# A transformer trunk with routed experts on one core: the 32-slot expert round moved into the last stored round, gate projections regrouped, filler matmuls added

## The reference, cut to what matters

```python
logits = (h @ router).astype(jnp.float32)
top_v, top_i = lax.top_k(logits, TOP_K)          # TOP_K = 2 of N_EXPERTS = 8
w = jax.nn.softmax(top_v, axis=-1)
combine = jnp.sum(jax.nn.one_hot(top_i, N_EXPERTS, dtype=jnp.float32) * w[..., None], axis=-2)
gu = jnp.einsum('btd,edf->btef', h, w_gu)        # w_gu: 8 x 1024 x 2816
g, u = jnp.split(gu, 2, axis=-1)
act = jax.nn.silu(g) * u * combine[..., None].astype(h.dtype)
return jnp.einsum('btef,efd->btd', act, w_down)  # w_down: 8 x 1408 x 1024
```

## Time and profile before

| | |
|---|---|
| median of 3 runs | 2147.89 us (2145.49 to 2149.15) |
| the profiled execution's own time | 2149.53 us |
| its span, first to last instruction | 2147.7 us |
| mean granted TensorE clock | 0.986 |
| busy: PE, PEld, DVE, ACT, POOL | 2078.1, 1535.5, 826.7, 381.4, 126.9 us |
| DMA | 550.71 MB, mean 256 GB/s |

### The profile page before, as it was taken

How to read it: one execution, slowest core, us unless ns; L and a number is a source line. 1 busy time by engine, 2 the same in 40 slices (tenths; PEclk the granted TensorE clock), 3 DMA queues, 4 the chain that set the end, 5 groups by cost and what they waited for, 6 DMA issues and landing times.

```text
span 2147.7 us, 44261 instructions
## 1 busy us (share of the span) xinstructions
PE 2078.1 (97%) x19281; PEld 1535.5 (71%) x19281; DVE 826.7 (38%) x1886; ACT 381.4 (18%) x816; POOL 126.9 (6%) x221
## 2 busy tenths in 40 slices
PE   6998999999999999999999999999998999999998
PEld 4776878888899655456587688888887876554564
DVE  2235753777575500101312345653336734001013
ACT  1124441000110110001132310001134331110010
POOL 3100010111000000000100011110000000000000
PEclk8999999999999999999999999999999999999999
DMA  9974039997546599999885799844441038999997
GB/s 337 280 261 138 13 100 323 349 298 265 195 154 221 204 367 401 397 393 398 301 246 189 256 341 293 284 127 139 137 137 56 13 102 325 365 400 399 394 394 266
DMA packets 376942, 550.71 MB, mean 256 GB/s; under 512 B 13104, under 2 KB 328880, under 8 KB 371424
## 3 DMA queue, kind: packets, MB, share of 16 engines
q1 hardware_dynamic: 349888, 466.59, 62.2%
q0 software_dynamic: 21968, 77.10, 10.8%
q10 hardware_dynamic: 4896, 4.21, 0.6%
HBM read 537.90 MB, written 14.67 MB: 257 GB/s over the span
## 4 chain that ended last, share of the span: by engine, by line
PE 88%; DVE 6%; DMA 2%; ACT 2%; issue 1%; ACTq 0%; SPq 0%; DVEq 0%
PE ps L731 85%; DMA work<-in_ada_w 2%; DVE ring L2270 1%; DVE ring L2264 1%; ACT ring L1670 1%; DVE ring L2245 1%; ACT work L1670 1%; DVE ring L2289 1%; DVE work L2103 1%; PE ps L1304 1%; PE ps L921 0%; DMA ring<-in_ada_w 0%; PE ps L1244 0%; PE ps L1190 0%; DVE ring L2278 0%
## 5 line engine op out<-in xcount | busy, mean ns | idle before, releaser
L731 PE MATMUL ps<-hT,ring 128*128 128x256 f32 (+1 forms) x2912 | 637.7, 377 | 2.8 <-DVE hT L2113 2.5
L731 PE MATMUL ps<-ring,work 128*32 128x352 f32 (+5 forms) x7320 | 618.3, 438 | 8.6 <-ACT work L1670 5.7
L731 PEld LDWEIGHTS ps<-hT,ring 128*128 128x128 f32 x2912 | 542.9, 192 | 102.9 <-issue 20.5
L731 PEld LDWEIGHTS ps<-ring,work 128*32 128x32 f32 (+2 forms) x7320 | 307.0, 116 | 291.6 <-issue 196.2
L1670 ACT ACTIVATE work<-ps 128x256 f32<-128x256 f32 (+13 forms) x244 | 104.6, 433 | 1254.9 <-PE ps L731 992.2
L731 PE MATMUL ps<-work,ring 128*128 128x256 f32 (+2 forms) x1664 | 322.0, 352 | 1.1 <-DVE work L2397 0.9
L731 PEld LDWEIGHTS ps<-work,ring 128*128 128x128 f32 (+1 forms) x1664 | 275.3, 187 | 35.6 <-issue 1.6
L2754 DVE SCALAR_TENSOR_TENSOR work<-work,csil 128x1024 f32<-128x1024 f32 x196 | 239.5, 1280 | 45.3 <-DMA work<-in_ada_w 45.0
L731 PE MATMUL ps<-ring 64*64 64x64 f32 (+1 forms) x4192 | 153.3, 235 | 18.4 <-DVE ring L2289 9.1
L2621 DVE TENSOR_TENSOR work<-work,ps 96x352 f32<-96x352 f32 (+2 forms) x72 | 37.4, 520 | 322.1 <-PE ps L731 321.6
L731 PEld LDWEIGHTS ps<-ring 64*64 64x64 f32 x4192 | 130.4, 139 | 33.1 <-DVE ring L2289 13.8
(11 more groups left out here) (294 smaller groups left out, 1253.4 us busy)
## 6 DMA issues: line engine op xcount, KB each, us to landing
ring<-in_moe_w_gu SPq DMA_DIRECT2D x128, 1408.0 KB, 13.8
work<-in_ada_w POOLq DMA_DIRECT2D x112, 512.0 KB, 6.3
ring<-in_moe_w_down SPq DMA_DIRECT2D x48, 1024.0 KB, 13.0
ring<-in_ff_w_gu SPq DMA_DIRECT2D x88, 512.0 KB, 7.8
ring<-in_ada_w SPq DMA_DIRECT2D x40, 1024.0 KB, 7.9
ring<-in_dn_w_in SPq DMA_DIRECT2D x32, 1024.0 KB, 5.5
ring<-in_moe_w_down SPq DMA_DIRECT2D x64, 512.0 KB, 11.3
ring<-in_ff_w_down SPq DMA_DIRECT2D x44, 512.0 KB, 8.9
```

What stands on the lines that cost most here:

```text
L731: return pe.matmul(out, lhsT, rhs, start=start, stop=stop, **kw)
```

## The change

The 32-slot round is computed inside the last stored round: its gate columns stand before down chunks 4 to 7, its up columns before chunk 8, its turn before chunk 9 and its down product after chunk 10. Its rows stay in the chip (`y_tiny`, `back_tiny`), and the 128-slot round's scatter adds them by a second matmul behind each of its own. The 32-slot expert is now fetched seventh, the 128-slot one eighth. `xg_tiny` and its copy go. The gate projection makes `wab` stationary in groups of 32 columns, `hT` moving, and a second step sums the groups (`fold`). One panel of the attention layer goes ahead of the scores' waits, and fillers are added at the start, in the router, and at the end of DeltaNet. The counts in the semaphore waits follow (not shown), as do a new constant, memory for it (`par` shrinks), and a clear of `y_tiny` at the end of `wide` on VectorE.

```diff
@@ SP: the order in which experts are fetched
-                    n_end = sp.snap(n_last + TINY)
+                    n_more = sp.snap(n_last + (NARROW - 1))
...
                     next_expert(NARROW - 3, LAST_LARGE, for_large)
-                    with sp.Fori(TINY, n_end) as r:
-                        next_expert(r, r + (NARROW - TINY), [0, 1, 2, 3, 4, 5, 6, 7])
-                    next_expert(n_end, TINY, [0, 1, 2, 3, 4, 5, 6, 7])
+                    next_expert(NARROW - 2, TINY, [0, 1, 2, 3, 4, 5, 6, 7])
+                    with sp.Fori(NARROW - 1, n_more) as r:
+                        next_expert(r, r + 1, [0, 1, 2, 3, 4, 5, 6, 7])
@@ TensorE: body, the last stored round
                     if upcoming is not None:
                         pe.wait_ge(moe["d_g"], upcoming + (i + 1))
                         gather(0, G_pair)
-                    down(q, 4, 8, 3, first)
-                    if upcoming is not None:
+                        down(q, 4, 8, 3, first)
                         gather(1, G_pair)
                         gather(2, G_pair)
-                    down(q, 8, 11, 4, first)
+                        down(q, 8, 11, 4, first)
+                    else:
+                        columns_tiny(q + 1, GATE, 0)
+                        down(q, 4, 8, 3, first)
+                        columns_tiny(q + 1, UP, 1)
+                        down(q, 8, 9, 4, first)
+                        turn_tiny(q + 1)
+                        down(q, 9, 11, 4, first)
+                        down_tiny(q + 1)
@@ TensorE: scatter of the 128-slot round
+                        r = slice(BLK * b, BLK * (b + 1))
                         for c in range(2):
                             k = 2 * b + c
-                            ins = mm(ps[:, b, c * NT:(c + 1) * NT], y_w[:, k * P:(k + 1) * P], back_T)
+                            mm(ps[:, b, c * NT:(c + 1) * NT], y_w[:, k * P:(k + 1) * P], back_T, True, False)
+                            ins = mm(ps[:, b, c * NT:(c + 1) * NT], y_tiny[r, c * P:(c + 1) * P], back_tiny[r, :], False, True)
@@ TensorE: the end of experts
                 with pe.Fori(0, n_last) as r:
-                    wide(q0 + STORED + r)
-                tiny(pe.snap(q0 + n_last + STORED))
+                    wide(q0 + NARROW + r)
@@ ScalarE: tiny, which now also has the last stored round's output and stores
                     ins.then_inc(moe["a_at"], 4)
+                    act.wait_ge(moe["p_bt"], q - (6 * i + 5))
+                    f(back_tiny[:], ps[:, 1, NT:2 * NT], ACT.Copy).then_inc(moe["a_bt"], 1)
+                    output(q - 1, STORED * (i + 1) - 1)
+                    store(q - 1, LAST_LARGE)
                     act.wait_ge(moe["p_dn"], q * 4 + 4)
@@ VectorE: tiny
                     ins.then_inc(moe["d_act"], 2)
+                    output(q - 1, STORED * (i + 1) - 1)
                     dve.wait_ge(moe["p_dn"], q * 4 + 4)
-                    cp(y_tiny[64:P, :], ps[64:P, 4, 0:QUARTER]).then_inc(moe["d_y"], 1)
-                    for b in range(4):
-                        dve.wait_ge(moe["p_sc"], (q - STORED * (i + 1)) * 4 + (b + 1))
-                        residual(l, b, b, 40, moe["d_res"])
+                    cp(y_tiny[64:P, :], ps[64:P, 6, 0:QUARTER]).then_inc(moe["d_y"], 1)
@@ TensorE: the gates of DeltaNet (gates_in after unit 1, gates_folded after unit 2)
                     pe.wait_ge(small_in, SMALL[l])
+                    for k in range(KC):
+                        q = slice(BLK * (k % 4), BLK * (k % 4 + 1))
+                        ins = mm(ps[q, 6, 0:NT], wab[:, k, :], hT[:, k, :], k < 4, k >= 4)
+                    ins.then_inc(p_ab, 1)
+
+                def gates_folded():
+                    pe.wait_ge(d_ab, i + 1)
                     for g in range(2):
-                        for k in range(KC):
-                            mm(ps[:, 6, 32 * g:32 * g + 32], hT[:, k, g * P:(g + 1) * P], wab[:, k, :],
-                               k == 0, k == KC - 1)
-                    mm(ps[:, 6, 64:96], ones[0:1, :], arow[0:1, :]).then_inc(p_ab, 1)
+                        mm(ps[:, 6, NT + 32 * g:NT + 32 * g + 32], GATES(l)[:, g * P:(g + 1) * P], fold)
+                    mm(ps[:, 6, NT + 64:NT + 96], ones[0:1, :], arow[0:1, :]).then_inc(p_ab, 1)
@@ VectorE: the copy between them (gates_in of VectorE goes from w == 2 to w == 3)
+                    if w == 1:
+                        dve.wait_ge(p_ab, 3 * i + 1)
+                        cp(GATES(l), ps[:, 6, 0:NT]).then_inc(d_ab, 1)
@@ TensorE: fillers; end of DeltaNet, router, start of layer 0
                     sums(l, 8 + m, 2 + m % 2, ones)
+                    keep_warm(6, 1)
...
+                    if k < KC - 1:
+                        keep_warm(0, 1)
                 ins.then_inc(moe["p_rt"], 1)
...
-                    for _ in range(EARLY):
+                    for x in range(EARLY):
                         ada(0, 1, ROWS512(0))
+                        if x >= EARLY - 3:
+                            keep_warm(6, 3)
...
                     ins.then_inc(p_pro, 1)
+                    keep_warm(6, 3)
                     ada_turn(1, ROWS512(0))
+                    keep_warm(6, 4)
@@ TensorE: attention, one panel (NA_FIRST = 1, NA_PANELS[0] from 1 to 0)
+                pe.wait_ge(d_ct, 2)
+                pe.wait_ge(d_ar, ada_turned[0])
+                for _ in range(NA_FIRST):
+                    ada(NA_ACC, NA_ACC, ROWS512(l, True))
                 pe.wait_ge(a_pj, PJ0[l] + 12)
```

More of the change, by code:

```diff
@@ L51 @@
 C_RCAP = C_CAP + 2 * P
-NCONST = C_RCAP + COLS
+C_FOLD = C_RCAP + COLS
+NCONST = C_FOLD + 32
 def shape_constants():
@@ L204, in trunk @@
         identc = cst[:, C_IDC:C_IDC + HB]
+        fold = cst[:, C_FOLD:C_FOLD + 32]
         def level(l):
@@ L355, in trunk @@
         NA_ACC = 7
-        NA_PANELS = [1, 3, 2, 2, 0, 3, 3, 2, 0, 0]
+        NA_FIRST, NA_PANELS = 1, [0, 3, 2, 2, 0, 3, 3, 2, 0, 0]
         NA_WARM = [0, 0, 0, 0, 0, 0, 0, 0, 0, 5]
         NA_DONE, NA_TURN = (3, 7), (4, 8)
-        assert sum(NA_PANELS) == NA_CORE
+        assert NA_FIRST + sum(NA_PANELS) == NA_CORE
         PJ0 = {0: 0, 1: 12, 2: 24, 3: 36}
@@ L1497, in turn_tiny @@
                 def turn_tiny(q):
-                    pe.wait_ge(moe["d_res"], (q - STORED * (i + 1)) * 4 + 4)
-                    pe.wait_ge(moe["d_bk"], q - (STORED * (i + 1) - 1))
+                    pe.wait_ge(moe["d_bk"], q - (6 * i + 5))
+                    pe.wait_ge(moe["d_act"], q * 4 + 2)
                     for g in range(2):
-                        ins = pe.transpose(ps[:, 1, g * P:(g + 1) * P], back[:, g, :], ident)
+                        ins = pe.transpose(ps[:, 1, NT + g * P:NT + (g + 1) * P], back[:, g, :], ident)
                     ins.then_inc(moe["p_bt"], 1)
-                    pe.wait_ge(moe["d_act"], q * 4 + 2)
-                    for x in range(4):
+                    for x in (2, 3, 0, 1):
                         n = min(P, REACH - x * P)
-                        ins = pe.transpose(ps[0:n, 0 if x < 2 else 5, x * P:(x + 1) * P], ma[:, x * P:x * P + n], ident)
+                        ins = pe.transpose(ps[0:n, x // 2, (x % 2) * P:(x % 2 + 1) * P], ma[:, x * P:x * P + n], ident)
                     ins.then_inc(moe["p_tr"], 4)
@@ L1516, in down_tiny @@
                         for g in range(4):
-                            ins = mm(ps[BLK * g:BLK * (g + 1), 4, 0:QUARTER], ma_tiny_T[:, c, :], quarter(c, g),
+                            ins = mm(ps[BLK * g:BLK * (g + 1), 6, 0:QUARTER], ma_tiny_T[:, c, :], quarter(c, g),
                                      n == 0, n == 10)
                         down_done(ins, n)
-                def scatter_tiny(q):
-                    pe.wait_ge(moe["a_bt"], q - (STORED * (i + 1) - 1))
-                    for b in range(4):
-                        pe.wait_ge(moe["d_y" if b >= 2 else "a_y"], q + 1)
-                        r = slice(BLK * b, BLK * (b + 1))
-                        for c in range(2):
-                            ins = mm(ps[:, b, c * NT:(c + 1) * NT], y_tiny[r, c * P:(c + 1) * P], back_T[r, :])
-                        ins.then_inc(moe["p_sc"], 1)
-                def tiny(q):
-                    pe.wait_ge(moe["d_xt"], i + 1)
-                    columns_tiny(q, GATE, 7)
-                    columns_tiny(q, UP, 6)
-                    turn_tiny(q)
-                    down_tiny(q)
-                    scatter_tiny(q)
                 def body(q, upcoming, first=False):
@@ L2012, in experts @@
                 body(STORED - 1, None)
-                output(q0 + (STORED - 1), STORED * (i + 1) - 1)
-                store(q0 + (STORED - 1), LAST_LARGE)
+                tiny(q0 + STORED)
                 act.wait_ge(moe["d_np"], i + 1)
@@ L2017, in experts @@
                 with act.Fori(0, n_last) as r:
-                    wide(r + STORED)
-                tiny(act.snap(q0 + n_last + STORED))
+                    wide(r + NARROW)
```

88 lines of the change are left out of this document (40 added, 48 removed).

## The result

The changed kernel takes 2190.35 us (median of 4 runs, 2187.69 to 2194.53) against 2146.71 of the kernel before (4 runs), ratio 1.0206, 95% interval 1.0192 to 1.0220. The forecast was 2169, range 2154 to 2182: the sign is right, the loss is twice as large (43.6 us for 21), and the time lies outside the range. The profiled execution has 2192.01 us and a span of 2190.2 us, 42.5 longer than before.

A forecast was written before the change was run, and what follows sets the result against it. TensorE and the DMA engines are both full, so the weights' lead and order count. The move adds 32.0 us (+15.3 layer 1, +16.7 layer 3), other edits -9.3: +22.7, 2172.2 profiled, rounded to 2169 as median; range 2154 to 2182.

The forecast's parts named there:

- First stall: Before the small round's gate columns: TensorE waits from 964.9 to 975.7 for the last gate piece, 10.8 us.
- Scatter 3.6 + 6.0 = 9.6: Common scatter: 6.0 us added for eight small matmuls and changes of tiling mode, bounds 1.2 and 6.0.
- The gates of layer 3: Regrouped gate projection in layer 3: -3.8 us, fully on TensorE's path.
- the panel ahead of the scores: Attention: one of 16 panels moves into the 0.94 us idle before the scores, -0.9 us.
- the wait for a late panel in layer 0: Unit 5's panel has less than 1 us of slack, so layer 0 gains 2.3 us of a possible 5.2.
- gate columns, half of 9.67 us, to 980.5; four of seven chunks, 5.3: After the first stall: gate columns end at 980.5, then four down chunks take 5.3 us, to 985.8.
- second stall: Before the small round's up columns: TensorE waits 4.5 us for the last up piece, landing at 990.3.
- the stalls cool TensorE: Rival: idle halves the clock, second and third stall then cost about 3 us each time: 2180, chance 0.12.
- SP waits on the last chunk before it issues the spares ... third stall 2.3: Small downs: spares issued at 999.8 with the queue drained, landing at 1007.5; TensorE waits 2.3 us.
- the wide round's first gate piece ... so no stall, with about 1 us to spare: Start of the 128-slot round: first gate piece lands at 1011.2, gather ends at 1012.5, so no stall.
- router fillers: ... so I take -0.8 and -0.2: Routers: seven fillers, 3.2 us of work, avoid half clock; -0.8 and -0.2 us in the two layers.
- The pieces are there: Rival: gate pieces land 10.8 us earlier, so TensorE's work alone sets the time: 2132, chance 0.06.

The follow-up runs named there:

- e4_warm: Changed kernel with filler matmuls (22 and 6 of 256 columns) in the first two stalls: 2186.37 us.
- e5_late: Changed kernel with the 32-slot round's gate columns after down chunks 4 to 7 and up columns after chunk 10: 2179.2 us.
- e11_light_late: Changed kernel loading one of eight row blocks of the 32-slot expert's column pieces, its columns placed later among the down chunks: 2143.61 us, ratio 0.9979 to the kernel before.
- e2_move: The moved round alone on the kernel before, with the old gates and no fillers: 2191.27 us, ratio 1.0196.
- e13: Kernel before with regrouped gates, early panel, fillers at start, DeltaNet's end and the 32-slot round's gaps, none in the router: 2134.36 us, ratio 0.9936.
- e14: Changed kernel without the router's fillers: 2185.78 us, 4.6 less than the changed kernel.
- e1_rest: All edits except the moved round, on the kernel before: 2142.71 us, ratio 0.9966.
- e15: As e13, with two of the seven router fillers, behind the third and sixth pair of matmuls: 2139.4 us.

## Why the prediction was wrong in size

The mechanism held, three terms of the sum did not: the columns behind the stalls were taken at full clock, the 128-slot round was given no stall, and the router's fillers were taken to pay.

**Right.** The bound and its mechanism: the small round's weights are its successor's no longer but the next in the queue, and no edit brings them sooner. First stall 10.8 forecast, 10.99 and 10.79 measured. Scatter 3.6 + 6.0 = 9.6, measured 9.92; the price of a change of rows, 0.15 us from the attention's scores, is 0.20 here. The Trainium skill's TensorEngine Tiling (Array Packing), Key Properties, says that a change of the tiling mode drains the engine; the trace agrees in that each change costs 0.20 us. The gates of layer 3 (-3.0 for -3.8), the panel ahead of the scores (-0.8 for -0.9) and the wait for a late panel in layer 0, which takes back much of what the start gains, were as worked out; the stretch up to layer 1 ended 1.3 us short of its term.

**Wrong, the step "gate columns, half of 9.67 us, to 980.5; four of seven chunks, 5.3" and the same for the up columns.** They were taken at full clock. Measured: 12.12 for 10.1 and 9.17 for 6.1 us in layer 1; in layer 3 11.72 for 10.1, and 5.46 for 3.84 in the gather. The second stall gives part back (3.06 and 2.70 for 4.5). In layer 1's sum this is the largest term, 5.1 us less 1.4; in layer 3 the columns come out even and the gather's 1.6 stays. This was my rival "the stalls cool TensorE", with 0.12; it is true for the first stall, and e4_warm prices it for both layers at 4.0 us by the medians, 6.6 in the traces' stages. It should have been in the sum, since the rows of the start showed a half clock for 13.7 us. What stood before those was not "mostly idle time", as the rival says, but waits of 0.83 and 2.42 us in a stretch where TensorE was busy 7.75 of 11 us.

**Wrong in part, the step "SP waits on the last chunk before it issues the spares ... third stall 2.3".** The waits measure 4.2 and 4.5 us a layer. The spares themselves land 8.1 us after their first issue, for 7.7 (layer 1); they are issued 2.5 us late, nearly all of it from the slow columns before. The waits are longer mostly because the small downs between them took 5.3 us and not 6.6, a saving that I had said the stall would swallow. From the start of the turn to the gather the sum is short by only some 1 us a layer. What the step overlooks is that slot 10 waits for chunk 8 just so. It also says that the queue has drained by then, and charges nothing for it to the round behind: in layer 1 6.5 us of transfer time. What e5_late (11.1 us) and e11_light_late (10.2) regain is the worth of a better order, part of which my sum already counted as loss (the first stall without cover, the spares behind it); it is not a measure of this miss.

**Wrong, "the wide round's first gate piece ... so no stall, with about 1 us to spare".** It stalls 1.75 and 2.13 us, in layer 3 with 1.7 us at a lower clock behind it. The pieces start later by the drained stretch and share the queue with the row fetch; which of the two decides is not shown (e2_move stalls 0.33 and 0.25 us there with the same fetch). The slack of 1 us was within the error of the steps before it.

These terms make up most of the way from +15.3 to +22.3 in layer 1 and from +16.7 to +22.9 in layer 3.

**Wrong, the step "router fillers: ... so I take -0.8 and -0.2".** Measured +0.5 and +2.4, the second near the upper bound of 3.2 that I had given. I argued that the work is paced by vectors, so fillers would fit in the gaps; the bare router has no gaps for them, and each filler adds 0.36 us. e13 and e14 show it, with 5.9 and 4.6 us by the medians and 4.3 and 3.3 in the traces' routers.

**The rivals.** "The pieces are there" (2132) can be compared with e11_light_late, which has that state: 2143.6. Of the 11.6 us, 3.9 are the routers (+2.9 where I had -1.0) and 4.6 are two waits a layer for vectors at the small turn (0.93 and 1.35 us in layer 1, 0.8 and 1.5 in layer 3) that I had left out; the other 3.1 are not placed. So even with almost free weights the move gains nothing over e1_rest (2142.71): the idle time around the old small round goes, but a longer scatter and these waits take its place.

The transfers ran at 397 to 407 GB/s through the first two stalls. The Trainium skill's DMA: Bandwidth & Descriptors (Where 436 GB/s comes from) gives about 358 GB/s as the limit of HBM for a core, which is half of what the two cores of a stack share. This one core, with no other running the program, was above it in the trace. At the 435 GB/s of the rival the seventh expert would come 17 us earlier by the same estimate (185.7 us of transfers at 395 GB/s), not 20; the conclusion stays.

What is left open: the gates gain 4.9 us by the ratio and 3.2 by the trace, and e13_best 5.9 by the median where the routers explain 4.3 (2.2 in each layer); both differences are within the intervals. No kernel that fetches the 32-slot expert at another place than seventh or eighth was tried.

## What to carry to other kernels

When compute and transfers are both full, the order of the rounds is a schedule of bytes: a round with full weights and a quarter of the work must not stand where its predecessor hasn't built up a lead. Before moving work ahead of an instruction that frees a buffer, list what waits for that buffer: here the late release cost 10 us in two stages even when the expert's bytes were few, and no single wait shows it. A filler paid here in waits of 11 us for a transfer; in a chain of short steps it was added to each.

## What had not been expected of the hardware

- TensorE's granted clock fell to 1.2 GHz behind 11 us of idle time and cost 2 us in 12; fillers kept it at 2.4 GHz and shortened the same instructions from 12.12 to 10.12 us. Behind the 3 us stall it fell in some stages and not in others, without fillers in any.
- It also fell without any wait: in e5_late's layer 1 it was granted 0.50 from 1072 to 1080 us, TensorE busy without a gap since 1015.26; the scatter took 13.96 us there for 9.92.
- Where the clock falls in a loosely filled stretch changes with edits far from it: bare routers in layer 1 took 20.5 (twice), 21.0, 22.6 and 24.3 us in five kernels with the same instructions there, and the two fillers of e15 came with the slowest of all, 24.9 us.
- A 32-row matmul of 256 columns costs 0.43 us behind another of its kind on the same rows, as a full one does, and 0.63 us behind a 128-row one (the 0.43 is the 1.06 us of a pair less 0.63).

The fastest kernel of this study is e13_best, 2134.36 us: the kernel before with its 32-slot round last, the regrouped gates, the early panel, the fillers at the start and at DeltaNet's end, fillers in the small round's gaps and none in the router.
